# Output projection and MLP of a transformer block in one program block, with the MLP's first weight sums, operand sums and splits placed between the last five output steps

## The reference, cut to what matters

```
x  = x + g1 * (mix @ w_out)                      # mix: 2048 x 1024, w_out: 1024 x 1024
h2 = rmsnorm(x, norm2_g) * (1 + sc2) + sh2
ff = square(relu(h2 @ w_ff1)) @ w_ff2            # w_ff1: 1024 x 4096, w_ff2: 4096 x 1024
x  = x + g2 * ff
return rmsnorm(x, final_g)
```

## Time and profile before

| | us |
|---|---|
| median of 3 runs | 3818.01 (3815.83 to 3818.86) |
| the profiled execution, its time | 3819.69 |
| its span, first to last instruction | 3817.9 |
| busy: TensorE | 3334.3 (87%) |
| busy: VectorE | 2477.1 (65%) |
| busy: ScalarE | 1839.2 (48%) |
| the output block, first transposes to last store issued | 2271.43 to 2501.96 |
| the MLP, first load issued to the end | 2505.03 to 3817.9 |

### The profile page before, as it was taken

One profiled execution on the slowest core, in us unless ns is written; L12 is line 12 of the kernel. 1 busy time (PEld: TensorE's weight loads), 2 busy tenths in 40 slices (PEclk: granted clock), 3 DMA queues, 4 the chain that ended last, 5 costly groups with the idle time before them and its releaser, 6 DMA issues. The chain is left out here.

```text
span 3817.9 us, 45207 instructions
## 1 busy us (share of the span) xinstructions
PE 3334.3 (87%) x15964; PEld 2646.3 (69%) x15964; DVE 2477.1 (65%) x4707; ACT 1839.2 (48%) x3059; POOL 355.9 (9%) x564
## 2 busy tenths in 40 slices
PE   8589688799897689878779969959998999999998
PEld 3478566677676467666567748848877887888877
DVE  1431388887884477776766637767788776555676
ACT  0321277787673588778876653322223222322232
POOL 0000011110010110000000000001111220000141
PEclk9699899899897699998889989979999999999999
DMA  8323333222233532111101024455454445764565
GB/s 309 116 85 111 108 104 104 91 89 78 67 127 113 160 114 74 51 44 44 43 28 35 23 87 148 144 173 175 152 170 149 152 154 182 242 231 144 193 219 194
DMA packets 339279, 480.15 MB, mean 126 GB/s; under 512 B 29346, under 2 KB 218946, under 8 KB 338516
## 3 DMA queue, kind: packets, MB, share of 16 engines
q1 hardware_dynamic: 295172, 329.39, 27.3%
q0 software_dynamic: 43888, 147.93, 10.8%
HBM read 320.23 MB, written 156.98 MB: 125 GB/s over the span
## 5 line engine op out<-in xcount | busy, mean ns | idle before, releaser
L1973 PE MATMUL m_ps<-m_h,w_hi 128*128 128x512 f32 x1792 | 561.1, 395 | 55.0 <-DVE w_lo L1700 18.6
L1973 PEld LDWEIGHTS m_ps<-m_h,w_hi 128*128 128x128 f32 x1792 | 341.2, 191 | 130.3 <-issue 35.3
L843 DVE SCALAR_TENSOR_TENSOR rank<-spare,iw,rank 128x1024 f32<-128x1024 f32 (+5 forms) x330 | 332.2, 1021 | 70.2 <-ACT spare L772 65.1
L1984 PE MATMUL m_ps<-w_hi,a_hi 128*128 128x512 f32 x896 | 350.7, 391 | 11.9 <-DVE w_lo L1856 8.9
L1973 PE MATMUL m_ps<-m_h,w_lo 128*128 128x512 f32 x896 | 352.8, 394 | 0.0
L1984 PE MATMUL m_ps<-w_lo,a_hi 128*128 128x512 f32 x896 | 350.2, 391 | 0.0
L1984 PE MATMUL m_ps<-w_hi,a_lo 128*128 128x512 f32 x896 | 350.1, 391 | 0.0
L772 ACT ACTIVATE spare<-isps 128x1024 f32<-128x1024 f32 (+5 forms) x352 | 280.3, 812 | 116.0 <-PE isps L740 80.1
L740 PE MATMUL isps<-ki,iq_hi 128*128 128x512 f32 (+3 forms) x608 | 239.9, 395 | 88.0 <-ACT spare L772 66.1
L2527 ACT ACTIVATE pt<-tps 128x512 f32<-128x512 f32 (+1 forms) x432 | 233.3, 572 | 113.3 <-PE tps L2466 56.2
L2466 PE MATMUL tps<-ident,probs 128*128 128x128 f32 x1632 | 239.7, 288 | 44.5 <-DVE probs L2682 28.2
(11 more groups left out here) (264 smaller groups left out, 7068.3 us busy)
## 6 DMA issues: line engine op xcount, KB each, us to landing
w_raw<-in_w_ff SPq DMA_DIRECT2D x136, 512.0 KB, 5.6
dram_aop<-a_out POOLq DMA_DIRECT2D x224, 256.0 KB, 2.4
a_lo<-dram_aop SPq DMA_DIRECT2D x56, 1024.0 KB, 5.9
ada_w<-in_w_ada SPq DMA_DIRECT2D x12, 2048.0 KB, 9.0
q_hi<-dram_proj_hi SPq DMA_DIRECT2D x128, 128.0 KB, 3.0
q_lo<-dram_proj_lo SPq DMA_DIRECT2D x128, 128.0 KB, 3.0
iq_hi<-dram_proj_hi SPq DMA_DIRECT2D x224, 64.0 KB, 2.5
iq_lo<-dram_proj_lo SPq DMA_DIRECT2D x224, 64.0 KB, 2.5
```

The costliest lines, as they stand in the source:

```text
L843: nc.vector.scalar_tensor_tensor(out=dst, in0=got, scalar=w, in1=dst, op0=ALU.mult, op1=ALU.add).then_inc(s_acc, 1)
L1973: mm = nc.tensor.matmul(ps[:, b], w[:, m % WOPS, k, :], hop[:, j, h, :, k, :], start=fresh and k == 0 and i == 0, stop=k == KH - 1 and i == 2,
L1984: mm = nc.tensor.matmul(ps[:, t], a[:, c % RING, k, t * P:(t + 1) * P], w[:, c % RING, k, :], start=first and i == 0, stop=last and i == 2 ...
```

## The change

It puts `output` and `mlp` into one function and one block, `output_mlp`. There is no meeting of the engines between them; in its place stand waits on single semaphores. The buffers of the output step are laid over those of the MLP so that `w1_raw`, `w1_sums`, `h_sums`, the split weights and A11's raw slot lie where `wo_raw` and a gap have been, and can be filled in the last steps. The two halves of each `m_h` slot change places (raw and lo first, hi second), so that A11's hi part lies on `wo_hi` and is written once the last output product is done. PSUM banks are shared in the same way.

A function `early(t)` on each engine runs ahead of step t:

```diff
-        def steps(eng, step, weights=None):
+        def steps(eng, step, weights=None, early=None):
...
             for t in range(LOOP_END, LAST + 1):
+                if early is not None:
+                    early(t)
                 step(t, t % 2)
...
+                def early(t):
+                    if t == 12:
+                        sp.wait_ge(s_wl, KT)
+                        load_w1(0)
+                        load_slot(0, P_A11, 0, 0)
+                    if t == 13:
+                        load_sums(0)
+                    if t == 14:
+                        load_w1(1)
+                        sp.dma_start(g2[:], bc(scr.gates[1])).then_inc(q_g, 16)
+                    if t == NB:
+                        sp.wait_ge(s_o, NB)
+                        load_slot(0, P_S2, 0, 0)
+                        load_slot(0, P_A12, 0, 1)
+                        load_slot(0, P_S4, 0, 1)
+                steps(sp, step, early=early)
                 for slot in range(2):
                     sp.wait_ge(s_xo[slot], 16 * (NB // 2))
-                    sp.wait_ge(s_so[slot], 16 * (NB // 2))
+                load_slot(0, P_A22, 1, 1)
...
+                def early(t):
+                    if t == 13:
+                        w1_hi(0, 0)
+                    if t == 14:
+                        w1_hi(0, 1)
+                        w1_hi(0, 2)
+                    if t == 15:
+                        w1_hi(0, 3)
+                    if t == NB:
+                        h_hi(0, P_A11)
+                steps(act, step, weights, early)
...
+                        if isinstance(t, int) and t == NB:
+                            h_low(0, P_A11)
                         dve.wait_ge(s_ss, t)
...
+                def early(t):
+                    if t == 13:
+                        w1_sums12(0)
+                        w1_low(0, 0)
+                    if t == 14:
+                        w1_low(0, 1)
+                        w1_low(0, 2)
+                    if t == 15:
+                        w1_low(0, 3)
+                        w1_sum3(0)
+                        sum_s1(0)
+                steps(dve, step, weights, early)
...
+                def early(t):
+                    if t == NB:
+                        product(0, 0)
+                steps(pe, step, early=early)
```

More of the change, by code:

```diff
@@ new lines, in output_mlp @@
+        with ExitStack() as banks:
+            ps = banks.enter_context(nc.psum_tensor("m_ps", [P, 8, GT], F32))
+        mps = ctx.enter_context(nc.psum_tensor("mps", [P, DM], F32))
+        ops = ctx.enter_context(nc.psum_tensor("ops", [P, 2, DM], F32))
+        hps = ctx.enter_context(nc.psum_tensor("hps", [P, DM], F32))
+        s_c = sem("s_const_in")
+        s_gc = sem("s_head_gains")
+        s_g1 = sem("s_gate_in")
+        s_w = [sem(f"s_wo_in{n}") for n in range(2)]
+        s_wh = sem("s_wo_hi")
@@ new lines, in output_mlp @@
+        s_wl = sem("s_wo_lo")
+        s_in = [sem(f"s_mix_in{n}") for n in range(2)]
+        s_xin = [sem(f"s_x_in{n}") for n in range(2)]
+        s_vm = sem("s_head_chain")
+        s_vx = sem("s_x1_chain")
+        s_hs = sem("s_head_scale")
+        s_sq = sem("s_head_squares")
+        s_q = sem("s_quotient")
+        s_r = sem("s_root")
+        s_m = sem("s_mix_ready")
+        s_mt = sem("s_mix_transposed")
+        s_mh = sem("s_mix_hi")
+        s_ml = sem("s_mix_lo")
+        s_o = sem("s_out_products")
@@ L1313, in mlp @@
+        s_x1 = sem("s_x1")
+        s_ss = sem("s_x1_squares")
+        s_var = sem("s_x1_variance")
+        s_std = sem("s_x1_std")
+        s_xn = sem("s_x1_normed")
+        s_ht = sem("s_h2_transposed")
+        s_hu = sem("s_h2")
+        s_xo = [sem(f"s_x1_stored{n}") for n in range(2)]
+        s_so = [sem(f"s_h2_stored{n}") for n in range(2)]
         q_h = [sem(f"s_h_in{n}") for n in range(7)]
@@ L1350, in mlp, with there @@
         q_o = sem("s_out_stored3")
+        def there(tile, least=0):
+            return not isinstance(tile, int) or least <= tile < NB
+        def steps(eng, step, weights=None, early=None):
+            for t in range(FIRST, LOOP):
+                if t == 0 and weights is not None:
+                    weights()
+                step(t, t % 2)
+            with eng.Fori(LOOP // 2, LOOP_END // 2) as pair:
+                for slot in range(2):
+                    step(pair * 2 + slot, slot)
+            for t in range(LOOP_END, LAST + 1):
+                if early is not None:
+                    early(t)
+                step(t, t % 2)
         def h_lo(j):
-            return hop[:, j, 1]
+            return hop[:, j, 0]
         def w1_part(n, j):
@@ L1755, in _ @@
                 h_low(0, P_A22)
+                for slot in range(2):
+                    dve.wait_ge(s_so[slot], 16 * (NB // 2))
                 for n in range(NS):
```

507 lines of the change are left out of this document (221 added, 286 removed).

## The result

| | us |
|---|---|
| before, runs beside these | 3816.92, median of 4 (3811.99 to 3818.86) |
| after | 3792.55, median of 4 (3791.29 to 3797.25) |
| ratio | 0.9931, interval 0.9918 to 0.9944 |
| profiled execution after: time, span | 3791.68, 3789.9 |

To see where each microsecond is, I cut both executions at the first transposes of the output block (`mps`, 2271.43 before, 2267.37 after), at the transposes that follow the last output product (called L: 2488.54 before, 2481.70 after), and at the start of product 2.

What follows compares the result with a forecast made beforehand. TensorE's products bound the kernel before and after the seam, something else inside it. Product 2's start moving from 2548.62 to 2529.1 gave 19.5 us less, so the median 3818.01 becomes 3798.5; range 3795.5 to 3803.5.

Steps and rivals of the forecast that it cites:

- what the new layout does: Swapped m_h halves, new addresses and waits on the residual: claimed to cost nothing if products keep their spacing.
- a rival in which the MLP becomes as slow as the output: MLP products slow to the output's spacing: 19.4 us lost in the first stage, 3837 if both; chance 0.02.
- Step 13 and the wait in step 14: Output steps: early weight work makes step 13's h 1.18 us late, so TensorE loses 0.8 us waiting for tile 15's mix.
- Steps 14 and 15: Last output steps: VectorE's added work is covered by idle time, so nothing is lost; without that cover up to 3.4 us.
- the prediction's own sign (more than 1 us): Output steps: the prediction is wrong if steps 14 and 15 are longer than 12.94 us by more than 1 us.
- Product 0: Seam: starts about 8.5 us behind the last output product after TensorE stands 7.4, and takes 5.26 at the low clock.
- Tile 15 and the chain: Seam: tile 15's h comes 4.8 us later than before; from it to product 2 take 25.0 us instead of 49.3.
- The loads: Seam: the MLP's first loads arrive in time, with a slack of 10 us or more.
- The late load: Seam: A22 arrives 15 to 20 us after its issue was due, giving 3803 to 3808; chance 0.08.
- no change: The gain is given back later in the MLP, leaving 3818; chance 0.02.
- the sign that 200 us no longer hold 884 products: MLP stages: the prediction is wrong if 200 us no longer hold 884 products.
- The last rival: Seam: product 0 can't start before tile 15's transposes, so tile 15 is 4 us earlier; about 3794.5; chance 0.01.

Runs made afterwards that it cites:

- e1: The kernel before with 32 unused bytes per partition ahead of mt_hi; 3811.47 us in one run, beside 3821.49 for the kernel before.
- e3: The changed kernel with 32 unused bytes ahead of mt_hi; 3800.71 us in one run.
- e7: The changed kernel with product 0 put behind the transposes of tile 15, its operands still early; 3790.72 us in one run.
- e6: The kernel before with 32 unused bytes ahead of wo_raw and 32 ahead of mt_hi; 3820.21 us in one run.
- e15: The kernel before with 128 bytes ahead of u in the input projection and 64 ahead of rank0 in the indexing stage; median 3813.33 us, ratio 0.9988.
- e16: The changed kernel with its seam's work reordered further, plus the two shifts of e15; 3774.53 us, ratio 0.9888 to the kernel before.
- e12: The changed kernel unaltered, timed again; 3795.31 us, ratio 0.9934 to the kernel before.
- e13: The kernel before with 160 bytes ahead of mt_hi; 3819.7 us in one run.
- e5: The kernel before with 32 unused bytes ahead of wo_raw alone, which moves both operands; 3818.72 us in one run.
- e10: The kernel before with 48 unused bytes ahead of mt_hi, which move it by 64; 3822.88 us in one run.
- e14: The kernel before with 96 bytes ahead of mt_hi; 3823.38 us in one run.
- e9: The kernel before with MLP first-stage weights moved 32 bytes, its operands 64, and the second stage's a_hi 64 further; 3852.74 us beside 3820.49.

## Why the prediction was wrong

**The step that failed** is the one on what the new layout does: "new addresses and the waits on the residual cost nothing if products keep their spacing". The products of the output did not keep it. The steps had been taken at 12.94 us after as before; they measured 12.64 to 12.75, and 16 of them gave 4.06 us (e1 alone, where nothing else differs). With this term in it the forecast is 3794.4, 1.9 us off, and the range moved by it holds the measured time. The prediction had seen the clue, 0.2334 us in the output against 0.2262 in the MLP for the same shape (0.2267 from start to start), and used it only for a rival in which the MLP becomes as slow as the output, at 0.02. The same mechanism could as well make the output as fast as the MLP, and it did. A difference between equal shapes that no row explains is a term with two signs.

The miss of 3798.5 against 3792.55, 5.95 us, falls apart like this: 4.06 for the spacing; 1.09 because the kernel before measured 3816.92 in this comparison, not 3818.01; 0.74 behind product 2, which is within that stretch's spread; 0.12 in the seam; less 0.48 for the wait of step 14; some 0.4 stay open. The low end of the range allowed 1 us for a faster product 0 and 1.5 for the spread of the runs (together 3796.0, where 3795.5 was given). The second was too small: three runs that span 3 us said little, when the kernel before spans 3811.99 to 3823.37 over all comparisons.

**Step 13 and the wait in step 14**: right in mechanism, 1.18 us of idle time instead of 0.8. VectorE's lateness is the same, but TensorE's steps are shorter, so it arrives earlier. With 12.94 us steps (e3) the step is 0.82 longer, as worked out.

**Steps 14 and 15**: right on the cover. Step 14 with the wait in it lasted 14.06 us, 1.12 over 12.94, so the prediction's own sign (more than 1 us) was there: the shorter steps make the same lateness of VectorE a longer wait. `xn` for tile 14 was done 2.75 us before its use (2478.95 to 2481.70), and 3.1 had been expected.

**Product 0**: right. It starts 8.36 us behind L (8.5 expected), TensorE stood 7.33 us (7.4), and it lasted 5.11 us to the transposes (5.26). The choice of the price at the low clock held; the granted clock was 0.50 from 2490 to 2494 us and rose in the last stretch, 0.77 from 2494 to 2496, as before.

**Tile 15 and the chain**: right. The last `h` is at L + 14.54 (14.8 expected), product 1 at L + 28.16 (28.4), and from `h` to product 2 are 25.12 us (25.0). The whole seam is 39.66 us; the prediction's numbers gave 39.8.

**The loads**: right. No engine waits for one behind tile 15; A22 goes out at L + 17.7, sooner than the 18.2 expected.

**The rivals**: the prediction reads TensorE as never stopping behind product 2 but once; it stops for 28.1 us in all there, but for 28.1 us after as well, so the sum is not touched by it. The late load, no change and a slower MLP did not occur; the sign that 200 us no longer hold 884 products stayed away as well, and it could not warn, for it looks at the MLP alone and the spacing changed in the output. The last rival, product 0 behind tile 15, was given 4 us of gain on tile 15; made into a kernel (e7) it gave 2.9, because A11's split stands ahead of `xn` there and the transposes come at L + 9.65, where before they came at L + 8.75.

## What to carry to other kernels

When tiles are laid out anew, work out the distance between the two operands that TensorE reads, in bytes of a partition, and keep it a multiple of 256: in this kernel the other distances tried cost 1 to 3% of the spacing of products, and a small tensor of a few bytes ahead of an operand is enough to lose or win it. Of work moved ahead of a seam ask which engine's chain sets the end: an early product on TensorE is worth nothing, and here cost 2.9 us, while it holds up the engine that makes the next operand. And read a single run by stretches between fixed points, since code that no edit touches can move the total by 10 us.

## What the runs showed of the hardware

All figures here are from start to start in the timelines, over stretches in which products of 512 columns stand back to back; the distance is the start of the operand of 128 columns less that of the operand of 512, and what counts is what it leaves over a multiple of 256 bytes.

| left over | us from start to start | where |
|---|---|---|
| 0 | 0.2266 to 0.2272 | output (after, e1, e6), both MLP stages (before, after), input projection and indexing (e15, e16) |
| 192 | 0.2289 | indexing (before, e12) |
| 128 | 0.2322 to 0.2325 | output (e13), input projection (before) |
| 32, 64, 224 | 0.2331 to 0.2334 | output (before, e3, e5, e10, e14), MLP stages of e9 (224 in the first, 64 in the second) |

The same distance gave the same spacing in different stages, and the price is not the same for all distances. None between 0 and 32 was tried. The granted clock was 1.00 in these stretches, so it is no matter of the clock. The Trainium skill, "TensorE: Matmul & The Clock Gate", section "Wait — 56ns, not 53.3ns?", gives 215.7 ns from start to start for 512 columns at 2.4 GHz; the fast spacing here is 11 ns above that, the slow one 18. Its page "SBUF — State Buffer", section "Operand start alignment", asks only for a multiple of the element's size and says of itself that this is about legality, not speed; the runs here show a price on speed. Why the distance matters, no run here tells.
